# Experts 1 to 7 sorted by their token counts on the chip, with 96 or 64 slots

## The reference

```
logits = v @ router                                # 256 x 8
top_val, top_idx = top_k(logits, 2); top_w = softmax(top_val)
for e in 0..7:  y += combine[:, e] * ((silu(v @ wg[e]) * (v @ wu[e])) @ wd[e])
                # wg, wu: 1024 x 2816, wd: 2816 x 1024, all float32
```

## Time and profile before

| | |
|---|---|
| median of three runs | 1570.85 us |
| the profiled execution | 1569.91 us, its span 1568.2 us |
| TensorE busy | 1537.9 us, 98% of the span |
| VectorE, ScalarE busy | 600.8 us, 465.2 us |
| DMA | 420.31 MB, mean 268 GB/s |
| experts | from 771 us to 1519 us of the span |
| one expert (1 to 6) | 93.4 us |

### The profile page before, as it was taken

One profiled execution on the slowest core, in us unless ns is written; L12 is line 12 of the kernel. 1 busy time (PEld: TensorE's weight loads), 2 busy tenths in 40 slices (PEclk: granted clock), 3 DMA queues, 4 the chain that ended last, 5 costly groups with the idle time before them and its releaser, 6 DMA issues.

```text
span 1568.2 us, 33642 instructions
## 1 busy us (share of the span) xinstructions
PE 1537.9 (98%) x15282; PEld 1181.6 (75%) x15282; DVE 600.8 (38%) x831; ACT 465.2 (30%) x659; POOL 63.2 (4%) x101
## 2 busy tenths in 40 slices
PE   8999999999999999999999999999999999999987
PEld 7887888888888888788867677677766767777666
DVE  5787878555556777788210000000000000000025
ACT  5656434544455556434300000000000001000024
POOL 3100000000000100000000000000000000001001
PEclk9999999999999999999999999999999999999999
DMA  8445446565555445454999999999999999999940
GB/s 294 145 151 162 157 140 195 188 193 188 188 189 170 146 160 163 135 183 168 364 354 393 394 353 409 344 408 382 372 407 341 409 355 394 394 357 409 396 145 28
DMA packets 163396, 420.31 MB, mean 268 GB/s; under 512 B 16818, under 2 KB 42212, under 8 KB 163252
## 3 DMA queue, kind: packets, MB, share of 16 engines
q1 hardware_dynamic: 159168, 407.69, 71.6%
q0 software_dynamic: 2432, 8.65, 1.6%
q10 hardware_dynamic: 1652, 1.80, 0.4%
HBM read 413.23 MB, written 4.85 MB: 267 GB/s over the span
## 4 chain that ended last, share of the span: by engine, by line
PE 97%; ACT 1%; DVE 1%; DMA 0%; POOL 0%; issue 0%; SPq 0%; POOLq 0%; ACTq 0%; DVEq 0%
PE ps L2018 42%; PE ps L1561 15%; PE ps L1563 14%; PE ps L1562 14%; PE ps L2059 2%; PE ps L1660 1%; PE ps L2085 1%; PE ps L1621 1%; PE ps L1807 1%; PE ps L1670 1%; ACT ffT_area L634 1%; DMA arena<-in_w_in 0%; PE ps L2088 0%; PE ps L2095 0%; PE ps L2009 0%; PE ps L1831 0%
## 5 line engine op out<-in xcount | busy, mean ns | idle before, releaser
L1561 PE MATMUL ps<-whi,ahi 128*128 128x512 f32 (+1 forms) x984 | 391.2, 398 | 4.6 <-DVE wlo L982 3.0
L1563 PE MATMUL ps<-wlo,ahi 128*128 128x512 f32 (+1 forms) x984 | 383.2, 389 | 0.0
L1562 PE MATMUL ps<-whi,alo 128*128 128x512 f32 (+1 forms) x984 | 382.6, 389 | 0.0
L982 DVE TENSOR_TENSOR wlo<-arena,whi 128x1024 fp32r<-128x1024 f32 (+1 forms) x246 | 289.0, 1217 | 83.9 <-ACT whi L634 83.0
L634 ACT ACTIVATE whi<-arena 128x1024 fp32r<-128x1024 f32 (+1 forms) x246 | 245.6, 1053 | 99.9 <-PE ps L1563 89.1
L1476 DVE TENSOR_TENSOR ff_area<-ff_area,ps 128x768 f32<-128x768 f32 x24 | 22.9, 954 | 642.4 <-PE ps L2018 642.4
L2018 PE MATMUL ps<-arena 128*32 128x512 f32 (+3 forms) x3816 | 267.1, 428 | 0.0
L2018 PEld LDWEIGHTS ps<-arena 128*32 128x32 f32 x3816 | 188.8, 110 | 63.7 <-issue 1.3
L1561 PEld LDWEIGHTS ps<-whi,ahi 128*128 128x128 f32 x984 | 184.9, 188 | 47.3 <-issue 9.0
L2018 PE MATMUL ps<-expert_ring,arena 128*32 128x256 f32 (+3 forms) x3096 | 217.1, 426 | 0.0
L1563 PEld LDWEIGHTS ps<-wlo,ahi 128*128 128x128 f32 x984 | 184.7, 188 | 38.9
(11 more groups left out here) (260 smaller groups left out, 920.0 us busy)
## 6 DMA issues: line engine op xcount, KB each, us to landing
arena<-in_w_in SPq DMA_DIRECT2D x112, 512.0 KB, 4.5
arena<-in_moe_wd SPq DMA_DIRECT2D x92, 512.0 KB, 7.5
expert_ring<-in_moe_wd SPq DMA_DIRECT2D x84, 512.0 KB, 7.5
arena<-in_moe_wu SPq DMA_DIRECT2D x76, 512.0 KB, 9.0
arena<-in_moe_wg SPq DMA_DIRECT2D x68, 512.0 KB, 8.5
expert_ring<-in_moe_wg SPq DMA_DIRECT2D x60, 512.0 KB, 8.3
expert_ring<-in_moe_wu SPq DMA_DIRECT2D x52, 512.0 KB, 9.9
arena<-in_moe_wu SPq DMA_DIRECT2D x36, 384.0 KB, 3.9
```

The source lines that it names most:

```text
L982: return V.tensor_tensor(dst, src, hi.bitcast(f32), ALU.subtract)
L1561: TE.matmul(o, ahi[:, sa], whi[:, sw], start=start, stop=False)
L1562: TE.matmul(o, alo[:, sa], whi[:, sw], start=False, stop=False)
L1563: return TE.matmul(o, ahi[:, sa], wlo[:, sw], start=False, stop=stop)
```

## The change

The work is now a list of eight *places*. Place 0 is expert 0 as before, with 96 slots. Places 1 to 7 take experts 1 to 7 in falling order of their token counts, which VectorE works out on the chip (`sort_experts`). Places 1 to 3 have 96 slots, places 4 to 7 have 64. SyncE loads the seven expert numbers into registers ahead of place 1's first granule, and the addresses of its DMAs from there on contain a register. With 64 slots a chunk takes four matmuls of 512 columns, one per band.

`biggest` becomes the largest excess of tokens over slots (the branch is taken above 0), and `pos_ready` is signalled at the end of the sorting. `RANK` says which sorted position a place takes.

Three more edits come along. One: in `MOE_ORDER` the third gate granule of the second and of the last third now stands ahead of a down granule (down 0, down 4). Two: three PLE granules are loaded ahead of the last eight expert granules, which then use arena buffers alone, and are split during the last five to seven granules of place 7. Three: place 7's y is copied out and spread at once (`combine_last`, four matmuls of 64 rows) instead of by blocks.

```diff
-NB = 3
-CAP = NB * Q
+NB = (3, 3, 3, 3, 2, 2, 2, 2)
+CAPS = [Q * n for n in NB]
+RANK = (7, 0, 1, 2, 3, 4, 5, 6)
...
-MOE_ORDER += [("gate", 1, 0), ("gate", 1, 1), ("down", 0, 0), ("gate", 1, 2), ("gate", 1, 3), ("down", 1, 0), ("up", 1, 0),
+MOE_ORDER += [("gate", 1, 0), ("gate", 1, 1), ("gate", 1, 2), ("down", 0, 0), ("gate", 1, 3), ("down", 1, 0), ("up", 1, 0),
...
+TAIL = 8
+LOADS = list(range(N_MOE - TAIL)) + [N_MOE + i for i in range(3)] + list(range(N_MOE - TAIL, N_MOE)) + [N_MOE + 3, N_MOE + 4]
...
+        free = [slot for slot in FREED if held[slot][-1] < N_MOE and (slot < ARENA_SLOTS or m < N_MOE - TAIL)]
+        slot = min(free, key=lambda slot: held[slot][-1])
...
+                return a[0, bass.ds(e, 1), rows, cols].rearrange("e k f -> (e k) f")
...
-            return eng.If(eng.value_load(biggest[0:1, 0:1]) > CAP)
+            return eng.If(eng.value_load(biggest[0:1, 0:1]) > 0)
...
-            for m in range(N_MOE + 5):
+            of_place = [0]
+            for m in LOADS:
+                if m == PER_E:
+                    sp.wait_ge(order_ready, 1)
+                    of_place += [sp.value_load(order[0:1, RANK[e]:RANK[e] + 1], min_val=0, max_val=NE - 1) for e in range(1, NE)]
...
-                            if e == NE - 1 and k >= PER_E - WR:
-                                convert(n + WR)
+                            if e == NE - 1 and PER_E - 7 <= k < PER_E - 4:
+                                convert(M0 + N_MOE + k - (PER_E - 7))
...
+                    def sort_experts():
+                        counts = sorting(COUNT, NE)
+                        link(V.tensor_copy(counts, bank(4, NE)))
+                        link(V.scalar_tensor_tensor(out=sorting(KEYS, NE), in0=counts, scalar=float(NE), in1=slots_iota[:, 0:NE],
+                                                    op0=ALU.mult, op1=ALU.subtract))
+                        link(V.memset(sorting(KEYS, 1), -1000.0))
+                        link(V.max(sorting(TOP_KEYS, NE), sorting(KEYS, NE)))
+                        V.max_index(order[:, :], sorting(TOP_KEYS, NE), sorting(KEYS, NE)).then_inc(order_ready, 1)
+                        dve.wait_ge(order_ready, 1)
+                        link(V.tensor_copy(sorting(SORTED, NE), order[:, :]))
+                        for e in range(NE):
+                            V.memset(sorting(CAP_R + RANK[e], 1), float(CAPS[e]))
+                            last = V.memset(sorting(ROW_R + RANK[e], 1), float(FIRST_ROW[e]))
+                        link(last)
...
+                        for dst, src in ((POS_R, by_tile(POS, 8, 16)), (ONE_R, one), (TWO_R, two)):
+                            for t in range(NT):
+                                link(V.tensor_tensor(product, is_at, src[:, t, :].unsqueeze(1).broadcast_to([P, NE, NE]), ALU.mult))
+                                link(V.reduce_sum(sorting(dst + NE * t, NE), product, AX.X))
...
+                        link(V.tensor_tensor(counts, counts, sorting(CAP_E, NE), ALU.subtract))
+                        link(V.reduce_max(wk(GAP + 48, 1), counts, AX.X))
+                        V.tensor_copy(biggest[:, :], wk(GAP + 48, 1)).then_inc(pos_ready, 1)
...
-                    link(V.reduce_max(wk(GAP + 48, 1), bank(4, 8), AX.X))
-                    V.tensor_copy(biggest[:, :], wk(GAP + 48, 1)).then_inc(pos_ready, 1)
+                    sort_experts()
...
+                    def combine_last():
+                        for t in range(NT):
+                            for half in range(2):
+                                rows = slice(64 * half, 64 * half + 64)
+                                last = TE.matmul(bank(LAST_BANKS[2 * t + half]), wk(XG + t * P, P)[rows], wk(YM, 512)[rows],
+                                                 start=True, stop=True)
+                        last.then_inc(last_combined, 1)
...
+                        if NB[e] == 2:
+                            for i in range(4):
+                                last = one(i, i % 2, bank(first, long), i // 2 * long, long, start)
+                            return last
                         for b in range(3):
                             one(b, b, bank(first, long), 0, long, start)
```

More of the change, by code:

```diff
@@ L17 @@
 Q = 32
-NB = 3
-CAP = NB * Q
+NB = (3, 3, 3, 3, 2, 2, 2, 2)
+CAPS = [Q * n for n in NB]
+RANK = (7, 0, 1, 2, 3, 4, 5, 6)
+FIRST_ROW = [sum(CAPS[:e]) for e in range(NE)]
 PLE = 256
@@ L377, in build, with row, tokens_x, x_half_of @@
         PT = (4096, 2048)
[L378 to L382, removed]
+        sil, ff = ff_area[:, 0:768], ff_area[:, 768:1536]
+        def row(e):
+            return 768 if NB[e] == 3 else 512
+        def tokens_x(e, chunk, n):
+            return wk(XG + (e % 2) * 768 + chunk * CAPS[e], n)
+        def x_half_of(e, half):
+            return tokens_x(e, 4 * half, 4 * CAPS[e])
         def tile_rows(i):
             return slice(Q * i, Q * i + Q)
[L387 to L393, removed]
+        def ffT(d, n=768, first=0):
+            return ffT_area[:, 768 * (d % 2) + first:768 * (d % 2) + first + n]
+        def rounds(e):
+            return NB[e] - 1
+        def round_no(e, d, n):
+            return sum(PAIRS * rounds(f) for f in range(e)) + d * rounds(e) + n
+        def sorting(first, n):
+            return ffT_area[:, 1536 + first:1536 + first + n]
+        def by_rank(first, e, t):
+            return sorting(first + NE * t + RANK[e], 1)
         LAST_BANKS = (0, 1, 4, 5)
+        KEYS, TOP_KEYS, SORTED, IS, PRODUCT, POS_R, ONE_R, TWO_R, SEL_R, COMB_R, CAP_R, ROW_R, CAP_E, COUNT = (
+            0, 8, 16, 32, 96, 160, 176, 192, 208, 224, 240, 248, 256, 264)
         def blocks(ap, m):
@@ L902, in _ @@
                             n = M0 + e * PER_E + k
-                            if kind == "gate" and part < 2 and j > 0:
+                            if kind == "gate" and part < rounds(e) and j > 0:
                                 ffT_out(e, j - 1, part)
@@ L1388, in rows_of_tokens @@
-                        for i, o in enumerate((one, two)):
+                        V.tensor_tensor(kept, ranked(POS_R), sorting(CAP_R, NE).unsqueeze(1).broadcast_to([P, NT, NE]), ALU.is_lt)
+                        link(V.tensor_tensor(base, ranked(POS_R), sorting(ROW_R, NE).unsqueeze(1).broadcast_to([P, NT, NE]), ALU.add))
+                        last_rank = RANK[NE - 1]
+                        link(V.memset(kept[:, :, last_rank:last_rank + 1], 0.0))
+                        for i, o in enumerate((ranked(ONE_R), ranked(TWO_R))):
@@ L1512, in _ @@
                 lo_of_transposes("ple", 1, r)
-                if layer == 1:
-                    convert(first - 1 + WR)
                 convert(first + WR)
@@ L2112, in _ @@
                                     pe.wait_ge(pos_ready, 1)
-                                up_granule(n, q, part, 0 if kind == "gate" else 4, WIDTHS[j])
-                                if kind == "gate" and part < 2 and j > 0:
+                                up_granule(e, n, part, 0 if kind == "gate" else 4, WIDTHS[j])
+                                if kind == "gate" and part < rounds(e) and j > 0:
                                     transpose_ff(e, j - 1, part)
```

257 lines of the change are left out of this document (124 added, 133 removed).

## The result

Changed kernel: **1525.2 us**, median of 3 runs (1524.5 to 1529.4), against 1570.85 before; ratio 0.9726, 95% interval [0.9701, 0.9751]. The forecast was 1519, range 1508 to 1542. The profiled execution took 1525.21 us, span 1523.3 (before 1569.91 and 1568.2), so the span fell by 44.9 us where 52.2 were forecast.

What follows compares the result with a forecast made beforehand. TensorE bounds the kernel, the DMAs close behind and, from place 4 on, ahead. The PLE product starts at 1476.5 instead of 1528.7, -52.2 us: span 1516.0, execution 1517.7, forecast 1519 us as that execution was 0.9 under the median; range 1508 to 1542.

Steps and rivals of the forecast that it cites:

- Start of place 4: End of expert 3, before at 1144.85: TensorE stays the bound, hidden 0.58 us waits save 4.6 us, so 1140.2.
- The stream: From place 4 on: after an 8.3 us landing, 132.0 MB at 409 GB/s take 322.7 us; last landing 1471.2.
- the gathers' price: GpSimd's three later gathers: counted in the stream as 0.26 MB each.
- the dry transfers behind the pause in place 7: Last eight granules, with four to seven buffers instead of 13: cost taken as nothing, bounds 0 to +4.
- From the last landing to the PLE product: End of place 7: last landing 1471.2, products end 1473.2, copy 0.8 us, spreading 2.5 us, PLE product starts 1476.5.
- The sorting: VectorE in place 0: takes 7.4 us, ready at 779, 2 us before TensorE needs it; bounds 0 and +5.
- The registers: SyncE ahead of granule 35: seven loads take 3.2 us once, covered by the buffers and by slack per place.
- TensorE's own part: Places with 64 slots: granules take 1.72 and 1.29 us, at most 65 us per place, 28.4 us less.
- The 0.79 MB granules: Places 4 to 7: running at 330 GB/s by themselves would cost 14.8 us more; taken near 0.
- 381 as ceiling: Rival, chance 0.12: DMAs reach only 381 GB/s and already bound the first four places; 1547 us.
- SyncE: Rival, chance 0.05: from granule 35 on, issuing DMAs with registers at 1.5 us each becomes the bound; 1625 us.
- The clock: Rival, chance 0.02: TensorE's clock stays down in the starved places, 121.8 us each; 1673 us.

Runs made afterwards that it cites:

- e3: Changed kernel with the gate granules again behind down 0 and down 4, the old order of granules: 1528.5 us.
- e1: The changed kernel run again unedited, as the base for the other runs: 1522.8 us.
- e10: Changed kernel with the token-row gather for the experts of places 5 to 7 left out but for one row: 1518.9 us.
- e2: Changed kernel with SyncE's registers for the order of experts replaced by constants, the sorting kept: 1523.1 us.
- e7: Changed kernel, second half of each down granule in places 4 to 7 fetched for 64 of 1024 columns, same number of DMAs: 1474.8 us.
- e8: e4 with the three PLE granules ahead of expert granules 20, 14 and 8 from the end, instead of all ahead of the last eight: 1515.5 us.
- e6: Changed kernel with half of TensorE's columns per matmul left out in places 4 to 7, same transfers: 1521.7 us.
- e11: e4 with four of the five PLE granules fetched behind the last expert granule, two conversions moved behind the experts' loop: 1509.4 us.
- e5: Changed kernel with 64 slots in the last place only, all other places with 96: 1538.4 us.
- e4: Changed kernel with places of 96 and 64 slots in turn instead of four large, then four small: 1515.4 us.
- e9: Changed kernel with the indirect token-row gather for the experts of places 5 to 7 replaced by a plain transfer of as many fixed rows: 1524.9 us.

## Why the prediction was right, and what it missed

The span was forecast at 1516.0 and came to 1523.3. The 7.3 us are made up so, by the prediction's own steps:

- **Start of place 4**: 1140.2 forecast, 1142.97 measured, +2.8. The step itself was right: places 1 to 3 last 92.2 us (forecast 92.3), as the wait of 0.58 us is gone, and e3 gives it back. The difference lies ahead of the experts, in code that the change doesn't touch: the first expert product starts at 774.08 instead of 770.87. The granted clock was 0.91 here in the first 20 us and 0.74 from 755 to 775, against 1.00 and 0.83 before. In e1 the copy that closes place 3 stands 4.0 us earlier: executions of the same kernel differ by this much (its clock was 1.00 and 0.83 in those two stretches). A forecast can't foresee that term.
- **The stream**: this is the term that was mis-sized. From place 4's start to the last landing 331.0 us were forecast and it took 336.5 (1142.97 to about 1479.5), +5.5. Behind the first 8.3 us the 132.0 MB went at 402 GB/s instead of 409:
```profile
1151.30:1479.50 328.20, 252.91 (x2234) 71.73 (x2226) 23.92 (x37) 22.80 (x37) 9.86 (x13) 0.98 1.02 402
```
  The 409 was the rate of windows in which nothing disturbs the stream, used as a mean over four places. Of the 5.5 us, e10 shows 2.8 as the gathers' price (2.3 at the least), which the sum had only as bytes. 2.0 are the dry transfers behind the pause in place 7; the prediction had bounded that at 0 to +4 and taken 0. The rest, 0.7 to 1.2, is open.
- **From the last landing to the PLE product**: 5.3 us forecast, 4.7 measured. The two halves of the spreading run side by side (1.9 us, where I took 2.5 between 1.7 and 3.4). The tail behind it is 39.1 us, 39.5 forecast.

Sum: 2.8 + 5.5 - 0.6 - 0.4 = 7.3.

What had been put at nothing cost nothing. The sorting took 6.0 us plus 0.15, against 7.4 forecast (memsets hardly count), and was ready at 780.8, 3.6 us ahead of the fifth granule. There is no gap on TensorE in place 0. The registers cost nothing (e2). TensorE's own part was forecast a little low: it is busy 67 us in places 5 and 6, where the prediction had at most 65 and "some 60"; behind the transfers that costs nothing. The 0.79 MB granules do not run at 330 by themselves: places 5 and 6 hold 404 GB/s with them.

The rivals. *381 as ceiling* fell with places 5 and 6 at 404. What the earlier trace rows showed as share 1.00 was not a limit of the transfers: the changed kernel shows 1.03 at 411. *SyncE* fell with 0.85 us per pair, with e2 and with e7. Issues do get longer while the queue is full (four took 4.31 us in place 4, and 4.45 in e2 with constants), so it is not the registers; I read it as waiting for the transfers ahead, since e7 is 48 us faster with as many issues. *The clock*: it stayed at 1.00 in places 5 and 6, with pauses of 0.5 to 1.8 us after nearly every granule. In place 7 the pause of 8.43 us halved it, and so did a shorter one before: behind 2.41 us of waiting a granule took 3.52 us, in a window with a granted clock of 0.57.
```profile
1446.24 3.52 PE L2081 MATMUL ps<-expert_ring,ffT_area 128*32 128x512 f32 x16 [2.41 <-DMA expert_ring<-in_moe_wd]
...
1446.00:1450.00 4.00, 3.76 (x24) 1.14 (x28) 0.00 (x0) 0.00 (x0) 0.00 (x0) 0.57 1.03 405
```
Length alone does not decide it: in e8 a pause of 2.42 us (at 1437) left the clock at 1.00.

The Trainium skill, "TensorE: Matmul & The Clock Gate", section "Loop structure matters more than you think", calls a loop with a long DMA wait between the matmuls bad because the array goes cold. The trace agrees for the 8.43 us, after which the clock was 0.52. The wait in the page's example is 8 us, and the prediction left out the word "long": the pauses of places 5 and 6 are not long, and there the clock stayed.

In e6, with half the columns in a granule, the clock fell to 0.70 to 0.79, and no loss came of it: 1521.7 us against 1522.8, since a stretch that the DMAs bind has time for slow products. What the low clock costs behind the long pause, where buffers are few, was not measured apart from the pause (e11).

What the prediction did not see is what the order of the places is worth. One small place behind the large ones has 13 granules lying ready and lasts 77.4 us instead of 92.2 (e5); each further one in a row spares TensorE 28 us and gives some 5, since the next bound stands right behind. Put in turn with large ones, the same eight places give 7.4 us more (e4), because the stream stays full from place 1 to the end of place 6. e11 takes out of the stream ahead of the last product what isn't needed before it, and shortens the pause.

## What to carry to other kernels

When two resources are both nearly full, price a change by the second one's bytes over its rate in windows where its queue is never empty, and count everything that shares the stream, the small gathers included. Expect a mean over a whole stage somewhat below that rate: here 402 to 404 GB/s against 409. If the change lightens the first resource in some stages only, put light and heavy stages in turn so that the buffers average them. Keep everything that isn't needed before the last product out of the stream ahead of it.

## What the runs showed of the chip

- A transfer of 64 rows (0.26 MB) by GpSimd's queue, indirect or plain, cost a full stream 0.8 to 0.9 us beyond its bytes (e10; e9 for the plain form, which dips alike).
- SyncE issues a pair of DMAs with addresses from registers in 0.85 us, with constants in 0.80 to 0.84; the time of the kernel is the same (e2).
- A granted clock of 0.70 to 0.79 over places 4 to 7, 338 us, cost nothing that can be seen where the DMAs were the bound (e6).
- A pause of 2.41 us was followed by half the clock, pauses of 0.5 to 1.8 us in places 5 and 6 were not (the changed kernel), nor was one of 2.42 us in e8.
- Sixteen memsets of one column in a row start 0.01 us apart, linked operations on 64 elements 0.26 us.
